# Two of each four gate rows on ScalarE, as gate * relu(1 - |column - slot|)

## The chip, the cores and the metric

The kernel runs on one core of one Trainium2 chip. The metric is device microseconds of one execution; lower is better. TensorE (PE) multiplies, VectorE (DVE) and ScalarE (ACT) work element by element, GpSimd (POOL) and SyncE (SP) here mostly start DMAs.

## The reference, cut to what matters

Two transformer blocks over 256 tokens of width 2048 are computed in float32. The second ends in a PEER layer: 8 heads choose 16 of 16,384 experts for each token (an expert number is a pair of key numbers from 0 to 127), and the chosen experts' outputs are summed with a softmax gate.

```python
def peer_ffn(h, w_pq, sub_keys, u_tab, v_tab):
    ...
    best, ci = lax.top_k(cand, PEER_TOPK)
    e1 = jnp.take_along_axis(i1, ci // PEER_TOPK, axis=-1)
    e2 = jnp.take_along_axis(i2, ci % PEER_TOPK, axis=-1)
    expert = (e1 * N_KEYS + e2).reshape(T, PEER_HEADS * PEER_TOPK)
    gate = jax.nn.softmax(best, axis=-1).reshape(T, PEER_HEADS * PEER_TOPK)
    ...
        act = jax.nn.gelu(jnp.einsum('cd,ckd->ck', hc, u), approximate=False) * gc
        vv = jnp.take(v_tab, ec, axis=0)
        return jnp.einsum('ck,ckd->cd', act, vv)
```

## The kernel before

The kernel gathers no experts. It computes all 16,384 of them in 8 groups of 16 tiles and multiplies each by a dense gate, which is zero for the experts that a token did not choose. The dense gates are built before that, in the gate loop, which is the subject here.

**What one group of the gate loop does.** For each token there are 128 chosen slots, one on each partition. `slot_T` holds them with the token along the free axis: part 0 is the first key number, part 1 the second, part 2 the gate. For a token, `hot_col` (128 slots x 128 columns) is 1 where the column equals key part 1, and `hot_row` is the gate where the column equals key part 0. Their product, a 128x128 matmul over the slots, is the token's 128x128 matrix of gates. The loop takes four tokens at a time, so it has 64 groups (n = 0 to 63), and everything in it is written out, not looped at run time:

- VectorE makes `hot_col[n % 2]` for four tokens in one instruction (L2214) and then the four `hot_row` rows in four instructions (L2219), each a comparison with one column of `slot_T` as a scalar and a multiplication by another. The last raises `hot_ready`. From n = 2 on it first waits for `hot_used`, that is until the matmuls of group n - 2 have read the same buffer.
- TensorE waits for `hot_ready` and for ScalarE's copy of group n - 2, runs four float32 matmuls (L1032; the trace counts eight, two passes each) into bank 3 or 4, and raises `hot_used`. While n is under 48 it then does one k-tile of an early expert tile (`whole_tiles`, L995, two passes) before the next group.
- ScalarE waits for `hot_used` and copies the bank to `g_stage` (L1408). After n = 15, 31 and 47 it also does the Gelu of an early expert tile (L1390). After n = 40 and n = 56 it splits two halves of a weight chunk into its high part (`split`, L1066, two instructions of 128x1024), and VectorE takes the low part of these after its groups n = 44 and 60 (`lower`, L1490, two instructions of 128x1024).
- GpSimd stores `g_stage` to DRAM every eight groups (L1473). When the last store has landed it loads the gates of the first expert group to `g_now` (L1477). VectorE's first product in the expert loop, `p_raw` (L2227), waits for that.

Ahead of the loop TensorE transposes the slots (L1021) and ScalarE copies them from the banks to `slot_T` in two instructions (L1399 and L1402). After the loop TensorE goes on with two chunks of the expert loop for which the weights are ready, and then waits for the chain that begins with `g_now`.

Each engine carries out its own instructions in the order written. The order across engines is set by semaphores only.

Of the kernel before, what the change touches and what calls it, by code (L numbers as in the profile page):

```python
# [9 lines left out]
ACT = mybir.ActivationFunctionType  # L10
# [3 lines left out]
P = 128  # L14
T = 256
# [170 lines left out]
def build(nc, a, out):  # L186
    with ExitStack() as ctx:
        def sb(name, shape, dt=F32, at=ctx):
            return at.enter_context(nc.sbuf_tensor(name, shape, dt))

        def sem(name):
            return ctx.enter_context(nc.semaphore(name))
# [15 lines left out]
        part = ExitStack()  # L208
        proj = sb("proj", [P, 44, T], at=part)
        bias = sb("bias", [P, HEADS1, T], at=part)  # L210
# [57 lines left out]


        sb("acc_again", [P, DT, T], at=part)  # L270
        slot_T = sb("slot_T", [P, 3, T], at=part)
        count = sb("count", [P, P + K_TOP], at=part)
        hot_row = [sb(f"hot_row{j}", [P, 4, P], at=part) for j in range(2)]
        hot_col = [sb(f"hot_col{j}", [P, 4, P], at=part) for j in range(2)]
# [27 lines left out]
        bank = [ctx.enter_context(nc.psum_tensor(f"bank{j}", [P, 512], F32)) for j in range(8)]  # L302
# [32 lines left out]
        sub_loaded, count_loaded, s3_done, acc_zero = (  # L335
            sem("sub_keys_loaded"), sem("count_loaded"), sem("scores3"), sem("acc_zero"))
        bank_read, best_ready, gate_exp, slots_done, slots_turned, turned_copied = (
            sem("scores3_read"), sem("best_less_max"), sem("gate_exp"), sem("slots_done"),
            sem("slots_transposed"), sem("slots_copied"))
        hot_ready, hot_used, gates_copied = sem("hot_ready"), sem("hot_used"), sem("gates_copied")  # L340
        gates_stored, g_loaded = [sem(f"gates_stored{j}") for j in range(2)], sem("gates_loaded")
        p_hi_done, p_lo_done = sem("p_hi_done"), sem("p_lo_done")
        cst2_loaded, dve_step, shift_step = sem("cst2_loaded"), sem("dve_step"), sem("shift_step")
# [29 lines left out]
        def pc(name, i=0, n=1):  # L373
            return par[:, PCOL[name] + i:PCOL[name] + i + n]
# [112 lines left out]
        def _(pe):  # L487
# [499 lines left out]
            def whole_tiles(x, k0, k1):  # L987

                c = N_PEER + x
                for k in range(k0, k1):  # L990
                    if k == 0 and x >= 2:
                        pe.wait_ge(gelu_done, FFN_Q * FQT + x - 1)
                    if k % 8 == 0:
                        pe.wait_ge(raw_loaded[c % 2][k // 8], 16 * (c // 2 + 1))
                    last = nc.tensor.matmul(bank[c % 2][:, 0:T], raw[c % 2][:, k * P:(k + 1) * P], h_f32[:, k, :],  # L995
                                            start=(k == 0), stop=(k == DT - 1))
                    if k % 8 == 7:
                        last.then_inc(half_done, 1)
# [27 lines left out]
            pe.wait_ge(turned_copied, 2)  # L1026
            for n in range(T // 4):
                pe.wait_ge(hot_ready, n + 1)
                if n >= 2:
                    pe.wait_ge(gates_copied, n - 1)  # L1030
                for x in range(4):
                    last = nc.tensor.matmul(bank[3 + n % 2][:, x * P:(x + 1) * P], hot_col[n % 2][:, x, :],  # L1032
                                            hot_row[n % 2][:, x, :], start=True, stop=True)
                last.then_inc(hot_used, 1)
                if n < (DT - EARLY) * DT:
                    whole_tiles(EARLY + n // DT, n % DT, n % DT + 1)
# [23 lines left out]
        def _(act):  # L1060
            def split(c, it, nk=DT):
                for part, (at, end) in enumerate(((0, HALF), (HALF, nk * P))):
                    act.wait_ge(raw_loaded[c % 2][part], it * 16 + (c // 2 + 1) * 16)
                    if c >= 2 or not isinstance(it, int):
                        act.wait_ge(half_done, it * 4 + (2 * c - 3 + part))
                    nc.scalar.activation(w_hi[c % 2][:, at:end], raw[c % 2][:, at:end], ACT.Copy  # L1066
                                         ).then_inc(hi_done, 1)
# [177 lines left out]
            for qh in range(16):  # L1245
# [4 lines left out]
                for tt in range(TT):  # L1250
                    x = 2 * qh + tt
                    nc.scalar.activation(prob2[qh % 2][:, tt, :], bank[3 + qh % 2][:, tt * T:(tt + 1) * T], ACT.Exp,
                                         bias=soft2[:, 0, x:x + 1], scale=0.125,
# [134 lines left out]
            def whole_gelu(x):  # L1388
                act.wait_ge(half_done, 2 * (N_PEER + x) + 2)
                nc.scalar.activation(u_act[:, x, :], bank[(N_PEER + x) % 2][:, 0:T], ACT.Gelu).then_inc(gelu_done, 1)  # L1390
# [9 lines left out]
                                 ).then_inc(turned_copied, 1)  # L1400
            act.wait_ge(slots_turned, 2)
            nc.scalar.activation(slot_T[:, 2, :], bank[6][:, 0:T], ACT.Copy).then_inc(turned_copied, 1)  # L1402
            for n in range(T // 4):
                b, at = n // 8, 4 * (n % 8)
                if b >= 2 and at == 0:
                    act.wait_ge(gates_stored[b % 2], 16 * (b // 2))
                act.wait_ge(hot_used, n + 1)
                nc.scalar.activation(g_stage[b % 2][:].rearrange("p g t e -> p t g e")[:, at:at + 4],  # L1408
                                     bank[3 + n % 2][:].rearrange("p (t g e) -> p t g e", t=4, e=K_TOP), ACT.Copy
                                     ).then_inc(gates_copied, 1)  # L1410
                if n % DT == DT - 1 and n < (DT - EARLY) * DT:
                    whole_gelu(EARLY + n // DT)
                if n in (FIRST_SPLIT, FIRST_SPLIT + 16):
                    split(N_PEER + DT + (n - FIRST_SPLIT) // 16, 0)
# [70 lines left out]
        def _(dve):  # L1485
# [7 lines left out]
            def lower(c, it, nk=DT, whole=0):  # L1493
                for part in range(2):
                    lower_part(c, it, part, nk, whole)
# [304 lines left out]
            n = prep.step(nc.vector.tensor_tensor(shift_c, pc("mu_prev", 0, 30), pc("mu_next", 0, 30), ALU.add))  # L1800
# [5 lines left out]
            n = prep.step(nc.vector.tensor_scalar(half_rk, pc("r_k", 0, 8), 0.5, None, ALU.mult))  # L1806
# [37 lines left out]
            for p in range(5):  # L1844
                if p + 1 < 5:
                    qk_mean(p + 1)
                x = proj2[:, 30 + 2 * p:32 + 2 * p, :]
# [23 lines left out]
            for qh in range(16):  # L1871
                m, x = qh // 2, 2 * qh
# [18 lines left out]
            for p in range(4):  # L1891
                x, ms = proj2[:, 30 + 2 * p:32 + 2 * p, :], q_ms[p % 2]
# [8 lines left out]
            def running_sum(m, d):  # L1901
                dve.wait_ge(affine_done, 2 * m + 1)
                return rw.step(nc.vector.tensor_tensor_scan(quad[1][:, d, :], reset, sig_w[:, d, :], 0.0,
                                                            ALU.mult, ALU.add))
# [22 lines left out]
            def kd_rows(m):  # L1927
                kd = bk[m % 3][:, 1, :, :]
                return rw.step(nc.vector.tensor_tensor(kd, kd, twice_of(8 + m), ALU.mult))
# [100 lines left out]
            for t in range(10):  # L2030
# [5 lines left out]
                for k in range(1, 6):  # L2036
# [3 lines left out]
                    if prepare and k == 1:  # L2040
                        n = running_sum(t, 1)
# [16 lines left out]
                    if prepare and k == 2:  # L2058
                        n = kd_rows(t)
# [30 lines left out]
            for p in range(4):  # L2090
# [3 lines left out]
                x, ms = proj2[:, 2 * p:2 * p + 2, :], q_ms[p % 2]  # L2094
# [3 lines left out]
                for t in (2 * p, 2 * p + 1):  # L2098
                    n = gn.step(nc.vector.tensor_scalar(proj2[:, t, :], proj2[:, t, :], pc("lnx_w", t), pc("lnx_b", t),
                                                        ALU.mult, ALU.add))  # L2100
# [110 lines left out]
            for n in range(T // 4):  # L2211
                if n >= 2:
                    dve.wait_ge(hot_used, n - 1)
                nc.vector.tensor_tensor(  # L2214
                    hot_col[n % 2][:], count[:, 0:P].unsqueeze(1).to_broadcast([P, 4, P]),
                    slot_T[:, 1, 4 * n:4 * n + 4].unsqueeze(2).to_broadcast([P, 4, P]), ALU.is_equal)
                for x in range(4):
                    t = 4 * n + x
                    last = nc.vector.tensor_scalar(hot_row[n % 2][:, x, :], count[:, 0:P], slot_T[:, 0, t:t + 1],  # L2219
                                                   slot_T[:, 2, t:t + 1], ALU.is_equal, ALU.mult)  # L2220
                last.then_inc(hot_ready, 1)
                if n in (FIRST_SPLIT + 4, FIRST_SPLIT + 20):
                    lower(N_PEER + DT + (n - FIRST_SPLIT) // 16, 0, whole=WHOLE)
# [150 lines left out]
```

## Time and profile before

| | |
|---|---|
| median of 3 runs | 4003.99 us (3989.61 to 4004.86) |
| the profiled execution's own time | 3994.76 us |
| its span in the profile | 3993.1 us |
| PE busy, share of the span | 3600.8 us, 90% |
| DVE busy | 2446.0 us, 61% |
| ACT busy | 1565.3 us, 39% |
| mean granted clock of TensorE | 0.939 of full speed |

Times are microseconds from the start of the span unless marked ns. PE is TensorE's matmuls and PEld its weight loads. Busy shares are means over stages with different limits. The gate loop lies between about 2498 and 2611.5 us, about 2.8% of the span, so what it costs is read from the rows of that stretch. The clock is given as a share of full speed: 1.0 is 2.4 GHz and 0.5 is 1.2 GHz.

### The profile page before, as it was taken

How to read it: one execution, taken by the hardware profiler on the slowest of the kernel's cores; microseconds unless marked ns; L12 is line 12 of the kernel's file. 1: busy time of each engine (PE TensorE's matmuls, PEld its weight loads, DVE VectorE, ACT ScalarE, POOL GpSimd, SP SyncE). 2: the span in 40 equal slices, each digit the busy share in tenths (PEclk: the TensorE clock that was granted, in tenths of full speed). 3: DMA queues.
4: the chain of work that ended last, by engine and by line, in shares of the span. 5: the costliest groups of instructions: out<-in, count | busy, mean ns of one | idle time of the engine just before them, and what ended most of it. 6: DMA issues, size and time to landing. Idle time of an engine off the chain costs nothing.

```text
span 3993.1 us, 71400 instructions
## 1 busy us (share of the span) xinstructions
PE 3600.8 (90%) x24910; PEld 3065.3 (77%) x24910; DVE 2446.0 (61%) x4140; ACT 1565.3 (39%) x2369; POOL 25.3 (1%) x40
## 2 busy tenths in 40 slices
PE   7996979999999799557786899889999999999998
PEld 5884768888888688236774787678888888888887
DVE  3464567676766675446554549955656565655665
ACT  3443344444444344232222330344535444444543
POOL 0000000000000000000000000000000000000000
PEclk8996989999999899559998999999999999999999
DMA  4551335556555355000000354456566565656564
GB/s 171 185 183 38 111 107 176 192 171 198 171 200 169 125 188 182 3 8 11 8 35 21 127 184 133 169 189 212 189 203 214 181 215 184 210 186 212 191 200 136
DMA packets 166200, 597.54 MB, mean 150 GB/s; under 512 B 18320, under 2 KB 26640, under 8 KB 164688
## 3 DMA queue, kind: packets, MB, share of 16 engines
q1 hardware_dynamic: 159600, 559.10, 43.0%
q0 software_dynamic: 6496, 36.96, 2.5%
q8 instruction: 76, 1.25, 0.1%
q14 instruction: 28, 0.23, 0.0%
HBM read 574.76 MB, written 20.97 MB: 149 GB/s over the span
## 4 chain that ended last, share of the span: by engine, by line
PE 81%; DVE 12%; ACT 3%; issue 2%; DMA 2%; DVEq 0%; SPq 0%; ACTq 0%; POOL 0%; POOLq 0%
PE bank L500 46%; PE bank L502 23%; PE bank L752 6%; DVE hot_row L2219 2%; PE bank L523 2%; DVE hot_col L2214 1%; PE bank L740 1%; PE bank L714 1%; PE bank L763 1%; DVE quad L1540 0%; ACT w_hi L1066 0%; PE bank L730 0%; DMA g_now<-gates 0%; DVE q_ms L1850 0%; DVE h_two L1530 0%
## 5 line engine op out<-in xcount | busy, mean ns | idle before, releaser
L500 PE MATMUL bank<-h_two,w_hi 128*128 128x512 f32 x5616 | 1973.2, 396 | 54.3 <-DVE h_two L1530 29.8
L502 PE MATMUL bank<-h_two,w_lo 128*128 128x256 f32 x5616 | 1576.7, 281 | 0.0
L1490 DVE TENSOR_TENSOR w_lo<-raw,w_hi 128x1024 fp32r<-128x1024 f32 (+1 forms) x1054 | 1224.8, 1185 | 224.0 <-ACT w_hi L1066 218.3
L500 PEld LDWEIGHTS bank<-h_two,w_hi 128*128 128x128 f32 x5616 | 1059.3, 189 | 304.6 <-issue 37.4
L1066 ACT ACTIVATE w_hi<-raw 128x1024 fp32r<-128x1024 f32 (+1 forms) x1054 | 1045.3, 1025 | 563.8 <-PE bank L502 524.5
L502 PEld LDWEIGHTS bank<-h_two,w_lo 128*128 128x128 f32 x5616 | 1067.6, 190 | 0.0
L500 PE MATMUL bank<-p_two,w_hi 128*128 128x512 f32 x1792 | 629.5, 394 | 2.5 <-DVE acc L1508 1.3
L502 PE MATMUL bank<-p_two,w_lo 128*128 128x256 f32 x1792 | 500.0, 279 | 0.0
L500 PEld LDWEIGHTS bank<-p_two,w_hi 128*128 128x128 f32 x1792 | 335.8, 187 | 86.8 <-DVE p_two L2233 5.6
L502 PEld LDWEIGHTS bank<-p_two,w_lo 128*128 128x128 f32 x1792 | 335.9, 187 | 0.0
L1504 DVE TENSOR_TENSOR acc<-acc,bank 128x256 f32 x192 | 81.0, 422 | 393.9 <-PE bank L502 393.9
L1071 ACT ACTIVATE stage<-bank 128x256 f32<-128x256 f32 x242 | 93.1, 385 | 479.7 <-PE bank L502 479.3
L500 PE MATMUL bank<-f_two,w_hi 128*128 128x512 f32 x704 | 252.0, 399 | 12.0 <-DVE f_two L1756 12.0
L1500 DVE TENSOR_TENSOR stage<-stage,bank 128x256 f32<-128x256 f32 x242 | 101.9, 421 | 218.7 <-ACT stage L1071 199.6
L502 PE MATMUL bank<-f_two,w_lo 128*128 128x256 f32 x704 | 201.8, 287 | 0.0
L500 PEld LDWEIGHTS bank<-f_two,w_hi 128*128 128x128 f32 x704 | 135.8, 193 | 42.3 <-DVE f_two L1756 13.2
L502 PEld LDWEIGHTS bank<-f_two,w_lo 128*128 128x128 f32 x704 | 136.6, 194 | 0.0
L995 PE MATMUL bank<-h_f,raw 128*128 128x256 f32 x512 | 120.1, 380 | 0.0
L523 PE MATMUL bank<-quad,cst 128*128 128x256 f32 x224 | 65.3, 462 | 51.0 <-ACT quad L1094 51.0
L995 PEld LDWEIGHTS bank<-h_f,raw 128*128 128x128 f32 x512 | 93.4, 191 | 10.4
L523 PEld LDWEIGHTS bank<-quad,cst 128*128 128x128 f32 x224 | 52.5, 238 | 63.1 <-ACT quad L1094 41.6
L1427 ACT ACTIVATE u_act<-stage 128x256 f32 x112 | 46.9, 419 | 136.2 <-DVE p_raw L2227 136.2
(328 smaller groups left out, 2865.5 us busy)
## 6 DMA issues: line engine op xcount, KB each, us to landing
raw<-in_u_tab SPq DMA_DIRECT2D x256, 512.0 KB, 3.9
raw<-in_v_tab SPq DMA_DIRECT2D x256, 512.0 KB, 4.4
raw<-in_w_up SPq DMA_DIRECT2D x176, 512.0 KB, 4.9
raw<-in_w_in SPq DMA_DIRECT2D x174, 512.0 KB, 4.3
raw<-in_w_out SPq DMA_DIRECT2D x64, 512.0 KB, 4.4
raw<-in_w_down SPq DMA_DIRECT2D x64, 512.0 KB, 3.5
raw<-in_w_pq SPq DMA_DIRECT2D x32, 512.0 KB, 4.4
gates<-g_stage POOLq DMA_DIRECT2D x8, 2048.0 KB, 8.5
```

Source lines behind the costliest of these rows:

```text
L500: nc.tensor.matmul(o[:], wh, two[:, k, :, :].rearrange("p a t -> p (a t)"), start=(k == 0), stop=False)
L502: last = nc.tensor.matmul(o[:, T:2 * T], wl, two[:, k, 0, :], start=False, stop=(k == nk - 1))
L523: last = nc.tensor.matmul(bank[2][:, 0:T], ones, quad[g % 2][:, k, :], start=(g == 0 and k == 0), stop=(g == groups - 1 and k == 3))
L752: return nc.tensor.matmul(o, lhs, rhs, start=start, stop=stop)
L995: last = nc.tensor.matmul(bank[c % 2][:, 0:T], raw[c % 2][:, k * P:(k + 1) * P], h_f32[:, k, :], start=(k == 0), stop=(k == DT - 1))
L1066: nc.scalar.activation(w_hi[c % 2][:, at:end], raw[c % 2][:, at:end], ACT.Copy).then_inc(hi_done, 1)
L1071: nc.scalar.activation(dst, bank[c % 2][:, 0:T], ACT.Copy).then_inc(copied, 1)
L1427: nc.scalar.activation(tile_of(u_act, i * 2 + j), stage[j][:], ACT.Gelu).then_inc(gelu_done, 1)
L1490: nc.vector.tensor_tensor(w_lo[c % 2][:, at:end], raw[c % 2][:, at:end], w_hi[c % 2][:, at:end].bitcast(F32), ALU.subtract).then_inc(lo_do ...
L1500: nc.vector.tensor_tensor(dst, dst, bank[c % 2][:, T:2 * T], ALU.add).then_inc(drained, 1)
L1504: nc.vector.tensor_tensor(dst, dst, bank[c % 2][:, 0:T], ALU.add).then_inc(acc_upper, 1)
L2219: last = nc.vector.tensor_scalar(hot_row[n % 2][:, x, :], count[:, 0:P], slot_T[:, 0, t:t + 1], slot_T[:, 2, t:t + 1], ALU.is_equal, ALU.mult)
```

## The change

Of each four rows of `hot_row`, VectorE keeps tokens x = 0 and 1. ScalarE builds x = 2 and 3, each in two instructions: `off = |column - slot|` (Abs, with the slot number as a bias read from `slot_T`, and scale -1) and then `relu(gate - gate * off)` (Relu, with a scale and a bias that are both read from `slot_T`). Since column and slot are whole numbers this is the gate where they are equal and zero elsewhere. A fourth part of `slot_T` holds the negated gate, from one more copy of the bank. The new semaphore `off_done` is raised by each of these instructions: ScalarE waits on it between its own steps, and TensorE waits for it before each group. ScalarE makes the rows of groups 0 and 1 ahead of its loop, and those of group n + 2 after its copy of group n.

```diff
-        slot_T = sb("slot_T", [P, 3, T], at=part)
+        slot_T = sb("slot_T", [P, 4, T], at=part)
+        off = sb("off", [P, 2, P], at=part)
...
+        off_done = sem("off_done")
...
             for n in range(T // 4):
                 pe.wait_ge(hot_ready, n + 1)
+                pe.wait_ge(off_done, 4 * n + 4)
...
             nc.scalar.activation(slot_T[:, 2, :], bank[6][:, 0:T], ACT.Copy).then_inc(turned_copied, 1)
+            nc.scalar.activation(slot_T[:, 3, :], bank[6][:, 0:T], ACT.Copy, scale=-1.0).then_inc(turned_copied, 1)
+            act.wait_ge(count_loaded, 16)
+            act.wait_ge(turned_copied, 3)
+
+            def gate_rows(n):
+
+                if n:
+                    act.wait_ge(off_done, 4 * n)
+                for x in (2, 3):
+                    t = 4 * n + x
+                    nc.scalar.activation(off[:, x - 2, :], count[:, 0:P], ACT.Abs, scale=-1.0, bias=slot_T[:, 0, t:t + 1]
+                                         ).then_inc(off_done, 1)
+                for x in (2, 3):
+                    t = 4 * n + x
+                    act.wait_ge(off_done, 4 * n + x - 1)
+                    nc.scalar.activation(hot_row[n % 2][:, x, :], off[:, x - 2, :], ACT.Relu,
+                                         scale=slot_T[:, 3, t:t + 1], bias=slot_T[:, 2, t:t + 1]).then_inc(off_done, 1)
+
+            gate_rows(0)
+            gate_rows(1)
             for n in range(T // 4):
...
                                      ).then_inc(gates_copied, 1)
+                if n + 2 < T // 4:
+                    gate_rows(n + 2)
...
-                for x in range(4):
+                for x in range(2):
                     t = 4 * n + x
                     last = nc.vector.tensor_scalar(hot_row[n % 2][:, x, :], count[:, 0:P], slot_T[:, 0, t:t + 1],
                                                    slot_T[:, 2, t:t + 1], ALU.is_equal, ALU.mult)
```

## Rows read from the trace of the kernel before

**Rows 1.** The page's chain that ended last, by engine

```profile
PE 81%; DVE 12%; ACT 3%; issue 2%; DMA 2%; DVEq 0%; SPq 0%; ACTq 0%; POOL 0%; POOLq 0%
```

**Rows 2.** The chain in order of time, 2494 to 2635: start, us, what

```profile
2512.70 0.60 DVE hot_col L2214
2513.30 1.03 DVE hot_row L2219 x4
...
2573.57 2.27 DVE w_lo L1490 x2
...
2611.91 7.50 DMA gates<-g_stage
...
2620.01 8.02 DMA g_now<-gates
```

**Rows 3.** Groups of instructions in 2497.5 to 2611: busy us, mean ns, idle before

```profile
L2219 DVE TENSOR_SCALAR hot_row<-count,slot_T 128x128 f32<-128x128 f32 x256 | 72.0, 356 | 0.0
...
L2214 DVE TENSOR_TENSOR hot_col<-count,slot_T 128x512 f32<-128x512 f32 x64 | 43.9, 686 | 3.5 <-ACT slot_T L1402 2.1 <-PE bank L1032 1.4
L1408 ACT ACTIVATE g_stage<-bank 128x512 f32<-128x512 f32 x64 | 38.2, 597 | 70.9 <-PE bank L1032 70.9
...
L1390 ACT ACTIVATE u_act<-bank 128x256 f32<-128x256 f32 x3 | 1.1, 378 | 0.0
```

**Rows 4.** Timeline of the gate loop: start us, us, engine, line, work

```profile
2497.61 0.38 ACT L1402 ACTIVATE slot_T<-bank 128x256 f32<-128x256 f32 x1
...
2501.97 0.60 ACT L1408 ACTIVATE g_stage<-bank 128x512 f32<-128x512 f32 x1 [3.98 <-PE bank L1032]
...
2504.47 0.60 ACT L1408 ACTIVATE g_stage<-bank 128x512 f32<-128x512 f32 x1 [1.90 <-PE bank L1032]
...
2509.50 1.16 PE L1032 MATMUL bank<-hot_row,hot_col 128*128 128x128 f32 x8
...
2511.13 0.97 PEld L1032 LDWEIGHTS bank<-hot_row,hot_col 128*128 128x128 f32 x8 [0.44 <-DVE hot_row L2219]
...
2568.74 1.99 ACT L1066 ACTIVATE w_hi<-raw 128x1024 fp32r<-128x1024 f32 x2
...
2610.87 0.60 ACT L1408 ACTIVATE g_stage<-bank 128x512 f32<-128x512 f32 x1 [0.51 <-PE bank L1032]
```

**Rows 5.** ScalarE's groups over the whole span, forms apart

```profile
L1313 ACT ACTIVATE rb<-bank 128x128 f32<-128x128 f32 x32 | 8.9, 278 | 70.0 <-PE bank L752 70.0
...
L1287 ACT ACTIVATE sig_w<-bank,small 128x256 f32<-128x256 f32 x16 | 6.7, 471 | 22.3 <-PE bank L763 22.3
...
L1297 ACT ACTIVATE bk<-sig_a,small 128x512 f32<-128x512 f32 x8 | 6.5, 813 | 0.3
...
L1304 ACT ACTIVATE decay<-quad 128x512 f32<-128x512 f32 x8 | 5.0, 619 | 0.0
...
L1141 ACT ACTIVATE prob<-logit,soft 128x128 f32<-128x128 f32 x8 | 3.1, 393 | 0.2 <-DVE soft L1602 0.2
...
L1390 ACT ACT_TABLE_LOAD x2 | 2.6, 1283 | 0.0
```

**Rows 6.** ScalarE's timeline where instructions follow each other

```profile
1781.31 0.84 ACT L1287 ACTIVATE sig_w<-bank,small 128x256 f32<-128x256 f32 x2 [9.24 <-PE bank L763]
...
1785.19 0.81 ACT L1297 ACTIVATE bk<-sig_a,small 128x512 f32<-128x512 f32 x1
1785.90 0.61 ACT L1304 ACTIVATE quad<-quad 128x512 f32<-128x512 f32 x1
...
1844.93 0.56 ACT L1320 ACTIVATE uv<-bank 64x128 f32<-64x128 f32 x2 [1.16 <-PE bank L752]
```

**Rows 7.** Engines' busy time by stretch; TensorE's granted clock is third from last

```profile
2500.00:2504.00 4.00, 4.00 (x17) 3.82 (x18) 3.09 (x10) 0.60 (x1) 0.00 (x0) 0.50 0.01 4
...
2584.00:2598.00 14.00, 10.03 (x70) 8.51 (x71) 14.00 (x44) 5.71 (x10) 0.89 (x1) 1.00 0.76 272
```

## The prediction

> **What bounds the kernel now.** I read the chain that ended last first. By engine it is mostly TensorE, with 12% of VectorE [rows 1]. The chain in order of time shows where the edited lines stand in it: from about 2504 to 2607 us it is VectorE alone, `hot_col` and four `hot_row` instructions in turn [rows 2]. So in the gate loop VectorE sets the pace and the other engines follow. One group takes 0.60 + 1.03 = 1.63 us there, which is 0.257 us for each `hot_row` instruction. VectorE's low parts, 2.27 us for a pair, are in the chain too, twice. Behind the loop stand the store of the gates (7.50 us) and the load of `g_now` (8.02 us) [rows 2]. Whatever moves the last copy to `g_stage` moves these, and with them the end.
>
> The groups of instructions in the stretch show how much room the others have. VectorE has 3.5 us of idle time before `hot_col`. ScalarE is idle for 70.9 us, always until TensorE's matmuls are done, and its 64 copies take 597 ns each [rows 3]. TensorE is not far from its own limit: the gap in its weight loads is 0.44 us in a group of 1.63 [rows 4], so a group with its expert tile needs about 1.19 us at full clock.
>
> **The change on VectorE.** Two of four rows go: 2 x 0.257 = 0.51 us for a group, which leaves 1.11 us. TensorE's work does not change. If nothing else bound the loop, it would now run at some 1.2 us a group.
>
> **The change on ScalarE.** It adds four instructions of 128x128 to a group. The trace has no Abs and no Relu, so I price them by form.
> - Abs reads SBUF, with a bias that is read from a tile. The nearest form is L1141, an Exp of 128x128 from SBUF with such a bias: 393 ns [rows 5].
> - Relu has a scale and a bias that are both read from a tile. L1297 is such an instruction at 128x512: 813 ns. L1304, the same shape without either, takes 619 ns [rows 5]. Each operand of this kind therefore costs 97 ns, and Relu takes 393 + 97 = 490 ns.
> - Instructions that follow each other overlap. Two of L1287 at 471 ns each [rows 5] span 0.84 us, and L1304 begins 0.71 us after the start of an L1297 that lasts 0.81 [rows 6]. The overlap is 0.10 us in both, with operands from tiles. So the spacing is 0.29 us for Abs, 0.39 for Relu and 0.50 for the copy of 0.597.
> - The waits on `off_done` cost nothing in a steady group: the first Relu starts 0.58 us after the first Abs, which was done at 0.39; the second Relu needs the second Abs (done at 0.68) and starts at 0.97.
>
> A group on ScalarE: 0.50 + 2 x 0.29 + 2 x 0.39 = 1.86 us. That is more than VectorE's 1.63 was. **ScalarE becomes the bound of the loop**, and each group is 0.23 us longer than before. TensorE's 1.19 us and VectorE's 1.11 us lie below it. Nor does the ring of waits bind: the rows of group n + 2 are ready 1.96 us after the copy of group n began, the matmuls take 1.16 [rows 4], and 3.2 us for two groups is under 2 x 1.86.
>
> The Trainium skill has a price and a rule here ("ScalarE: Activation LUTs", sections "What ACT_TABLE_LOAD costs" and "Rules for kernel authors"). The price is 186 ns + 0.833 ns per column, 93 ns more for each operand from a tile, and 93 ns of overlap; an estimate by it is 1.88 us for the group, which would put 1 us on the sum. The rule sends relu, max, add and mul to VectorE; its ratio is stated for bf16, which no row here shows, but in float32 a row costs VectorE 0.257 us and would cost ScalarE 0.68.
>
> **Edits that cost nothing, and what hides them.** The extra copy to `slot_T` and the rows of groups 0 and 1 lie ahead of ScalarE's loop. The copies of groups 0 and 1 begin 2.50 us apart in before, at half clock [rows 4, 7], and the first begins 4.4 us after L1402. On ScalarE, the copy (0.38), two sets of rows at 1.46 us each and the waits between end at 2501.3, before the first group's matmuls do at about 2501.9. Group 0's rows are ready at 2497.61 + 0.28 + 0.38 + 0.03 + 1.46 = 2499.8, and its matmuls, which take some 2 us at half clock and end at 2501.9, need them about then. If this cover were gone it would cost about a microsecond, once. TensorE's extra wait costs nothing while its group is shorter than ScalarE's.
>
> VectorE's two low parts (4.5 us in before) go off the path: VectorE now idles 0.75 us a group, its rows are 1.2 us early, and the copy behind the matmuls has 0.5 us of slack, together more than 2.27. In their place ScalarE's own work is no longer hidden: two splits at 1.99 - 0.10 = 1.89 us [rows 4] and three Gelus at 0.378 - 0.10 = 0.28 us [rows 3], in all 3.8 + 0.8 = 4.6 us.
>
> **The sum**, from the start of L1402 to the end of the last copy. Before: 2610.87 + 0.60 - 2497.61 = 113.9 us [rows 4].
> - to the copy of group 1, set by TensorE at half clock: 2504.47 - 2497.61 = 6.9 us, unchanged
> - 60 groups to the copy of group 61: 60 x 1.86 = 111.6
> - splits and Gelus: 4.6
> - from there the rows of group 63 (1.96), its matmuls (1.16), its copy (0.60) and handovers: 3.8
>
> After: 126.9 us. The difference is +13.0 us, or 0.33%. Store and load follow unchanged, and TensorE's idle time ahead of `g_now` moves with them. Against the profiled execution's 3994.76 us this gives 4007.8. That execution lies 9.2 us under the median of the runs, so against the median I forecast **4017 us**.
>
> **The bounds.** Everything hangs on the spacing of ScalarE's small instructions, which counts 60 times. Low: if operands from tiles added nothing once pipelined, each would be spaced like the plain 128x128 of L1313, 0.278 - 0.10 = 0.18 us [rows 5]; ScalarE's group would be 1.22 us. High: no overlap at all, as in the two of L1320 that span 0.56 us [rows 6], with full durations 0.60 + 2 x 0.39 + 2 x 0.49 and small gaps: 2.45 us. I take 1.86, since the rows with such operands show the overlap, and L1320 writes other partitions in each of its two.
>
> **The rivals.**
> - *Faster (0.07).* Spacing at the low bound. Then TensorE and the handovers set about 1.22 us: 6.9 + 73.2 + 4.6 + 3.1 = 87.8, which is 26 us less, 3978 us. For it: VectorE is the bound, and half its row work goes. Against it: L1297 and L1287 keep their longer spacing. It decides below a spacing sum of 1.63 us for ScalarE's group; to be faster by over 0.5% it needs 1.32.
> - *The overlap is lost at the waits (0.14).* Three of ScalarE's four new instructions stand behind a wait on ScalarE's own semaphore, which no row shows with the wait already met. At 2.45 us a group: 60 x 0.59 = 35 us on top, 4052 us. From 1.98 us a group it is slower by over 0.5%.
> - *The clock falls (0.08).* TensorE works 1.16 us in a group of 1.86 from n = 48 on, 62%, where it was busy for 72% at full clock before [rows 7]. At half clock a group with its expert tile takes 2.50 us [rows 4]. Half the time at that clock until n = 47 adds 24 x 0.64 = 15 us: 4032. Against it: at 2.50 us TensorE is busy throughout, and the clock returns.
> - *Table loads (0.03).* A load is 1283 ns [rows 5]. If Abs and Relu needed another table than Gelu, the three Gelus would cost six loads, 8 us more (4025); if they needed one each, 128 loads, 164 us (4181). The skill's page (same title, section "Table sets: the hidden batching unit") states that relu and abs are in every set. No run here shows it yet.
> - *My forecast* has the remaining 0.68.
>
> **How the numbers follow.** About 0.5% (20 us) is what a measurement of this kernel can tell from no change. The forecast is +13 us with some 7 us either way from the spread of the runs, and leaves about 0.10 of its 0.68 beyond +20 us. Slower: 0.10, 0.13 of the lost overlap, 0.05 of the clock, 0.02 of the tables: 0.30. Faster 0.06. Within 0.5%: 0.64. The range of 8 in 10 runs from 4000, the forecast less the spread and a group of 1.75 us (-7 us), to 4040, which takes in the clock and two thirds of the lost overlap. The forecast alone spans 4006 to 4028.
>
> **What would show it.** In the profile of the changed kernel: ScalarE busy nearly throughout 2504 to 2624, copies to `g_stage` 1.86 us apart, Abs near 390 and Relu near 490 ns; the chain through ScalarE's rows in place of VectorE's; VectorE idle before `hot_col` for over 40 us; the low parts out of the chain and the splits in it; the last store of the gates 13 us later; no table load in the loop. Copies 1.2 us apart, or 2.4, or a clock of 0.5 in the loop would prove me wrong.

## The result

| | median | runs |
|---|---|---|
| before | 3999.48 us (3989.61 to 4007.9) | 12 |
| after | 4013.51 us (3999.14 to 4020.0) | 12 |

The ratio is 1.0032, with a 95% interval of 1.0018 to 1.0045. At 4000 us that is 13 us slower (7 to 18). The forecast was +13.0 us.

**The profile after.** The page's busy line and its chain by engine and line, to be read beside [rows 1]:

```profile
PE 3607.2 (90%) x24910; PEld 3071.3 (77%) x24910; DVE 2417.4 (60%) x4012; ACT 1645.8 (41%) x2626; POOL 25.0 (1%) x40
...
PE 81%; DVE 10%; ACT 6%; issue 2%; DMA 2%; DVEq 0%; SPq 0%; ACTq 0%; POOL 0%; POOLq 0%
PE bank L502 45%; PE bank L504 23%; PE bank L754 5%; PE bank L525 2%; ACT hot_row L1421 1%; ACT off L1416 1%; PE bank L742 1%; PE bank L716 1%; ACT g_stage L1431 1%; ACT w_hi L1069 1%; PE bank L765 1%; DVE quad L1565 0%; DMA g_now<-gates 0%; PE bank L732 0%; DVE q_ms L1875 0%
```

VectorE lost 2 points of the chain and ScalarE won 3. VectorE's busy time fell by 28.6 us and ScalarE's rose by 80.5 us: work left the engine that set the pace of the gate loop, and more than that arrived on another. The chain in order of time, in the steady part of the loop (start, us, what), answers to [rows 2]:

```profile
2512.65 0.48 ACT g_stage L1431
2513.13 0.58 ACT off L1416 x2
2513.71 0.77 ACT hot_row L1421 x2
2514.48 0.48 ACT g_stage L1431
...
2582.89 1.89 ACT w_hi L1069 x2
...
2629.11 7.49 DMA gates<-g_stage
...
2637.19 8.73 DMA g_now<-gates
```

Where `hot_col` and `hot_row` of VectorE stood, every piece is now ScalarE's: copy 0.48, two Abs 0.58, two Relu 0.77, together 1.83 us a group. The split of a weight chunk stands in the chain, VectorE's low parts do not. The waits in the stretch of the loop (who waited for whom: us in total, times, longest) show the slack of the others:

```profile
DVE hot_col L2239 <- PE bank L1035: 41.5, 60, 1.7
...
ACT g_stage L1431 <- PE bank L1035: 2.6, 6, 0.8
```

ScalarE's wait ahead of its copies fell from 70.9 us [rows 3] to 2.6. VectorE waits 41.5 us for TensorE, where it had waited 1.4 of its 3.5 us [rows 3].

**How the runs are compared.** The two profiled executions differ by 21.1 us, but the code ahead of the loop is the same in both and already differs by 4.6 us: L1402 of before, L1405 of after, starts at 2497.61 and at 2502.19. In the experiments below it starts anywhere from 2487.8 to 2507.4. From the end of the last copy to the end of the span it is 1381.6 us before and 1385.5 after, and between 1381.7 and 1384.4 in the experiments, without relation to how long their loops are. So from a profile I use only the length of the loop, from that start to the end of the last copy, and for the whole kernel the ratio of many runs. The loop took 113.9 us before and 2628.66 - 2502.19 = 126.5 us after, 12.6 us more.

### The profile page after: what moved, and what is told of

It reads as the page before. It is cut to its first block, busy times and chain, and to the rows that moved or that the text cites. A ratio compares the mean times of both kernels' runs of the same rounds, so it can differ in the third digit from the quotient of the medians.

```text
span 4014.2 us, 71531 instructions
## 1 busy us (share of the span) xinstructions
PE 3607.2 (90%) x24910; PEld 3071.3 (77%) x24910; DVE 2417.4 (60%) x4012; ACT 1645.8 (41%) x2626; POOL 25.0 (1%) x40
## 4 chain that ended last, share of the span: by engine, by line
PE 81%; DVE 10%; ACT 6%; issue 2%; DMA 2%; DVEq 0%; SPq 0%; ACTq 0%; POOL 0%; POOLq 0%
PE bank L502 45%; PE bank L504 23%; PE bank L754 5%; PE bank L525 2%; ACT hot_row L1421 1%; ACT off L1416 1%; PE bank L742 1%; PE bank L716 1%; ACT g_stage L1431 1%; ACT w_hi L1069 1%; PE bank L765 1%; DVE quad L1565 0%; DMA g_now<-gates 0%; PE bank L732 0%; DVE q_ms L1875 0%
## 5 line engine op out<-in xcount | busy, mean ns | idle before, releaser
L1069 ACT ACTIVATE w_hi<-raw 128x1024 fp32r<-128x1024 f32 (+1 forms) x1054 | 1045.3, 1025 | 564.1 <-PE bank L504 522.4
L1035 PEld LDWEIGHTS bank<-hot_row,hot_col 128*128 128x128 f32 x512 | 67.4, 204 | 47.6 <-issue 46.1
L1035 PE MATMUL bank<-hot_row,hot_col 128*128 128x128 f32 x512 | 77.0, 297 | 28.0 <-issue 19.8
```

## The experiments

The spacing is that of the copies to `g_stage` in the steady part. It and the loop length are from each kernel's one profiled execution; the ratios are of 4 to 12 runs of each kernel against 12 to 24 of before.

| kernel | us a group | loop, us | against before's loop | timed ratio (95% interval) |
|---|---|---|---|---|
| before | 1.63 | 113.9 | | |
| after | 1.83 | 126.5 | +12.6 | 1.0032 (1.0018 to 1.0045) |
| one row on ScalarE | 1.37 | 101.8 | -12.1 | 0.9965 (0.9955 to 0.9976) |
| three rows | 2.51 | 167.4 | +53.5 | 1.0118 (1.0104 to 1.0133) |
| Relu with immediates | 1.46 | 105.4 | -8.5 | 0.9972 (0.9960 to 0.9983) |
| third row on VectorE, unused | 1.83 | 126.3 | +12.4 | 1.0028 (1.0018 to 1.0039) |
| four more met waits | 1.83 | 126.7 | +12.8 | 1.0029 (1.0018 to 1.0040) |
| one row, Abs ahead | 1.37 | 100.9 | -13.0 | 0.9959 (0.9945 to 0.9972) |
| rows on both, ScalarE's unused | 1.83 | 124.3 | +10.4 | 1.0021 (1.0012 to 1.0031) |

In every row but one the loop's difference lies inside the interval of the timed ratio. With three rows it is 53.5 us, and the interval ends at 53.2. So the gate loop accounts for the differences as far as these runs can tell.

**One row on ScalarE.**

```diff
-                for x in (2, 3):
+                for x in (3,):
...
-                for x in range(2):
+                for x in range(3):
```

(twice in ScalarE's part, once in VectorE's; `off` and the counts of `off_done` follow)

> ScalarE makes one row of each four (x = 3), VectorE three. If ScalarE's spacing sets the loop of the changed kernel: ScalarE needs about 0.48 + 0.37 + 0.39 = 1.24 us a group (Relu must now wait for the only Abs ahead of it), VectorE 0.60 + 3 x 0.257 = 1.37 us, TensorE 1.19, so VectorE sets the pace again. The loop from the second copy to slot_T to the last copy takes 6.7 + 60 x 1.37 + 4.5 (low parts) + 3.3 = about 97 us, against 113.9 before and 126.5 with two rows: about 17 us or 0.4% faster than before. Rival, the handovers to ScalarE and the extra wait on TensorE cost the time, however many rows: still 1.8 us a group, slower than before. Rival, VectorE's rows do not matter at all: 1.63 us and no change.

The pace is VectorE's again, at 1.37 us, and the kernel is 0.35% faster than before. The loop is 5 us longer than I worked out. Three lines of its chain tell where half of that went:

```profile
2581.04 0.56 ACT g_stage L1431
...
2582.04 13.87 DMA gates<-g_stage
...
2595.93 0.60 ACT g_stage L1431
```

The store of eight groups took 13.87 us, and eight groups now take only 8 x 1.37 = 11. ScalarE had to wait 2.5 us for the buffer. In before the same store took 12.9 us, ScalarE came back to its buffer 13.7 us after the store began, and nobody waited. Of the rest, part is TensorE's clock, which is granted at 0.62 from 2596 to 2602, right after that wait; I did not take the remainder apart.

**Three rows on ScalarE.** The same edit with `(1, 2, 3)` and `range(1)`.

> ScalarE makes three rows of each four (x = 1 to 3), VectorE one. If each row costs ScalarE the spacing of an Abs and a Relu (0.29 + 0.385): 0.48 + 3 x 0.675 = 2.51 us a group, the loop about 167 us, 41 us more than with two rows and 54 us (1.3%) more than before. Rival, a fixed cost of the handover: 1.84 us stays, 0.3% slower than before.

2.51 us a group and a loop of 167.4 us, both as worked out. From two rows to three a group is 0.68 us longer, which is the price of a row: 0.29 for the Abs and 0.385 for the Relu. A fixed cost of the handover as the cause of the loss is ruled out.

**Relu with immediates.**

```diff
-                                         scale=slot_T[:, 3, t:t + 1], bias=slot_T[:, 2, t:t + 1]).then_inc(off_done, 1)
+                                         scale=-1.0).then_inc(off_done, 1)
```

> All instructions and waits of the changed kernel stay, but the Relu takes scale -1 and no bias instead of two operands read from slot_T, so the rows x = 2 and 3 hold no gates. If operands from tiles cost 97 ns each in the spacing: Relu is spaced 0.19 us instead of 0.385, a group takes 0.48 + 0.58 + 0.38 = 1.45 us, and the loop is 25 us shorter than with two rows, 12 us (0.3%) faster than before. Rival, the count of instructions and waits sets the spacing: 1.84 us a group stays, and 0.3% slower than before.

The timeline of ScalarE, first in the kernel after, then here:

```profile
2592.70 0.58 ACT L1431 ACTIVATE g_stage<-bank 128x512 f32<-128x512 f32 x1
2593.17 0.69 ACT L1416 ACTIVATE off<-count,slot_T 128x128 f32<-128x128 f32 x2
2593.76 0.87 ACT L1421 ACTIVATE hot_row<-off,slot_T 128x128 f32<-128x128 f32 x2
2594.53 0.58 ACT L1431 ACTIVATE g_stage<-bank 128x512 f32<-128x512 f32 x1
```

```profile
2531.24 0.63 ACT L1431 ACTIVATE g_stage<-bank 128x512 f32<-128x512 f32 x1
2531.72 0.74 ACT L1416 ACTIVATE off<-count,slot_T 128x128 f32<-128x128 f32 x2
2532.30 0.55 ACT L1421 ACTIVATE hot_row<-off 128x128 f32<-128x128 f32 x2
2532.70 0.63 ACT L1431 ACTIVATE g_stage<-bank 128x512 f32<-128x512 f32 x1
```

The starts are what to read. From the first Relu to the next copy, which is two Relus, it is 0.77 us with two operands from `slot_T` each and 0.40 us with none. So each operand costs (0.77 - 0.40) / 4 = 0.09 us of spacing. The number of instructions and waits is the same. With these operands the change is slower than before; without them, which leaves wrong gates in two of four rows, it is faster (0.9972). The loop came out 4 us longer than expected: a group took 1.46 us, a store was waited for (1.4 us), and groups 1 to 2 and 58 to 59 were 2.1 and 2.3 us apart.

**A third row on VectorE, unused.**

```diff
+                nc.vector.tensor_scalar(spare[:, n % 2, :], count[:, 0:P], slot_T[:, 0, 4 * n:4 * n + 1],
+                                        slot_T[:, 2, 4 * n:4 * n + 1], ALU.is_equal, ALU.mult)
```

> The changed kernel, and VectorE makes a third row of 128x128 again, into a tile that nobody reads. VectorE then has 1.37 us a group. If ScalarE sets the pace with 1.84 us, nothing changes: 1.84 us a group, 0.3% slower than before, VectorE idle 0.26 us less in each group. If VectorE or the ring through it still sets the pace, 0.257 us more in each of 64 groups, 16 us, 0.7% slower than before.

Nothing changes. VectorE's own timeline shows the row going into its idle time, which falls from 0.63 us a group in the kernel after to 0.37:

```profile
2530.42 0.69 DVE L2239 TENSOR_TENSOR hot_col<-count,slot_T 128x512 f32<-128x512 f32 x1 [0.63 <-PE bank L1035]
```

```profile
2531.48 0.69 DVE L2240 TENSOR_TENSOR hot_col<-count,slot_T 128x512 f32<-128x512 f32 x1 [0.37 <-PE bank L1036]
2532.09 0.34 DVE L2243 TENSOR_SCALAR spare<-count,slot_T 128x128 f32<-128x128 f32 x1
2532.35 0.60 DVE L2247 TENSOR_SCALAR hot_row<-count,slot_T 128x128 f32<-128x128 f32 x2
```

**More waits.** Ahead of each Abs and each Relu:

```diff
+                    act.wait_ge(count_loaded, 16)
```

> The changed kernel, and ahead of each Abs and each Relu of ScalarE one more wait, on a semaphore that has long been raised: four more waits a group. If waits that are met cost ScalarE nothing behind running instructions: 1.84 us a group as in the changed kernel, 0.3% slower than before. If they break the overlap of its instructions (0.1 us each) or take a turn of their own: 0.1 to 0.4 us more a group, 6 to 25 us, 0.5 to 0.9% slower than before.

1.83 us a group and the same loop. Four waits that are already met add nothing to the spacing here. That waits break the overlap was the largest of my rivals.

**ScalarE's rows made but not used.** VectorE makes all four rows (`range(4)`), TensorE's new wait on `off_done` is left out, and the Relu writes elsewhere:

```diff
-                    nc.scalar.activation(hot_row[n % 2][:, x, :], off[:, x - 2, :], ACT.Relu,
+                    nc.scalar.activation(spare[:, n % 2, x - 2, :], off[:, x - 2, :], ACT.Relu,
```

> VectorE makes all four rows as in the kernel before. ScalarE does the Abs and the Relu of two rows as well, but into a tile that nobody reads, and TensorE does not wait for it. If what counts is that ScalarE's instructions stand in one stream with its copies to g_stage: ScalarE's 1.84 us a group sets the pace all the same, the loop takes 126 us, 0.3% slower than before, as in the changed kernel. If the loss comes from the handover of the rows to TensorE or from its added wait: 1.63 us a group and the time of the kernel before. If taking rows off VectorE had still bought something: slower than the changed kernel.

Again 1.83 us a group, though no engine waits for the rows and VectorE has its old load. The waits in the loop now name the copy as what TensorE lacks:

```profile
PE bank L1035 <- ACT g_stage L1431: 21.1, 49, 2.6
```

So the loss comes through ScalarE's stream: its 1.35 us of rows stand between one copy and the next, and TensorE needs the copy to reuse its bank. This kernel has twice the rows of the kernel after on VectorE and one wait less on TensorE, and its groups take the same time: what was taken off VectorE bought nothing. The loop is 2.2 us shorter than after's. Its start is not (6.8 us to the copy of group 1, against 6.7), but its copies stay 1.83 us apart behind the splits, where those of after are up to 2.3 apart, which makes 1.5 us, and from the copy of group 61 to the end it takes 3.0 us against 3.8, as its last two copies follow each other with no matmul to wait for.

**One row, with the Abs a group ahead.** ScalarE's order after the copy of group n becomes the Relu of group n + 2 and then the Abs of group n + 3.

```diff
+                if n + 2 < T // 4:
+                    gate_row(n + 2)
+                if n + 3 < T // 4:
+                    distance(n + 3)
```

> One row on ScalarE as before, but its Abs is issued a group ahead, so that Relu never waits for the Abs directly in front of it. ScalarE then needs 0.48 + 0.29 + 0.39 = 1.16 us a group, VectorE still 1.37. If VectorE sets the pace with one row, nothing is won beyond 1 or 2 us where ScalarE catches up after its splits: ratio 0.996 to 0.997, as with one row. If ScalarE's wait for its own Abs sets the pace with one row: 0.08 us less a group, 5 us more gained.

The group stays at 1.37 us, so ScalarE's wait for its own Abs did not set the pace. The loop is 0.9 us shorter, and the ratio of 0.9959 cannot be told from that of one row. Its median is the lowest measured here, and it is faster than both given kernels. It waits 3.0 us for the store of the gates:

```profile
ACT g_stage L1433 <- DMA gates<-g_stage: 3.0, 1, 3.0
```

## Why the prediction was right

**The bound.** VectorE set the loop's pace before, and ScalarE does after, by its number of instructions and their spacing. One, two and three rows gave 1.37, 1.83 and 2.51 us a group; worked out were 1.37, 1.86 and 2.51. Only the 1.86 was worked out before any result; the other two used spacings measured in the kernel after. A third row on VectorE that nobody uses, and all four rows on VectorE beside ScalarE's load, show that VectorE's share has no effect once ScalarE sets the pace.

**The price of the operations the trace lacked.** Abs was priced by an Exp of the same shape with the same kind of bias, Relu by the step from an instruction with immediates to one with two operands from a tile at another width. Forecast spacings were 0.29 and 0.39 us; measured are 0.58 / 2 = 0.29 and 0.77 / 2 = 0.385. The copy was 0.48, not 0.50, which makes 1.83 of 1.86. The overlap held, as the rows of pairs with such operands said [rows 6]. The pair of L1320 that showed none was rightly set aside, though no run shows why it has none. The estimate by the Trainium skill ("ScalarE: Activation LUTs", section "What ACT_TABLE_LOAD costs"), 1.88 us, was 0.05 above.

**The hidden and the exposed work.** The chain has the splits on the path and no low part. The low parts were free, as forecast, but the splits cost more than their own 1.89 us: while ScalarE splits, TensorE runs out of rows, and its clock falls just after. At the second split TensorE waits 2.60 us for ScalarE's row. VectorE ends its low part at 2619.81, and even then it waits 1.17 us for TensorE before it can go on:

```profile
2618.90 3.88 PE L1035 MATMUL bank<-hot_row,hot_col 128*128 128x128 f32 x16 [2.60 <-ACT hot_row L1421]
...
2620.98 0.69 DVE L2239 TENSOR_TENSOR hot_col<-count,slot_T 128x512 f32<-128x512 f32 x1 [1.17 <-PE bank L1035]
```

At the first split TensorE waits 2.16 us in the same way. The windows of the kernel after (third from last is the granted clock) show what follows:

```profile
2512.00:2582.00 70.00, 59.17 (x380) 45.03 (x379) 45.85 (x114) 70.00 (x193) 4.51 (x5) 1.00 0.44 159
...
2588.00:2592.00 4.00, 4.00 (x24) 3.77 (x24) 2.36 (x6) 3.55 (x11) 0.00 (x0) 0.71 0.00 0
2592.00:2606.00 14.00, 9.34 (x64) 7.42 (x63) 9.17 (x24) 14.00 (x40) 0.89 (x1) 1.00 0.56 185
2606.00:2615.00 9.00, 5.65 (x40) 4.81 (x40) 5.87 (x16) 9.00 (x26) 0.89 (x1) 1.00 0.45 180
2615.00:2622.00 7.00, 4.23 (x22) 4.05 (x23) 5.20 (x11) 6.65 (x16) 0.00 (x0) 0.68 0.89 311
```

and the copies are further apart there:

```profile
2586.39 0.70 ACT L1431 ACTIVATE g_stage<-bank 128x512 f32<-128x512 f32 x1
...
2588.66 0.60 ACT L1431 ACTIVATE g_stage<-bank 128x512 f32<-128x512 f32 x1 [0.21 <-PE bank L1035]
...
2590.85 0.60 ACT L1431 ACTIVATE g_stage<-bank 128x512 f32<-128x512 f32 x1 [0.24 <-PE bank L1035]
```

2.27 and 2.19 us instead of 1.83, and 2.31 and 2.02 after the second split, together 1.5 us. This is the rival of the clock in small. In the steady part it did not come: the clock stayed at 1.0 from 2512 to 2582 and from 2592 to 2615, and in the last of these windows TensorE's matmuls are on for 5.65 of 9 us, 63%, where the prediction had 62%.

**The sum**, term by term: to the copy of group 1 it took 6.7 us (forecast 6.9); from there to the copy of group 61 it took 2624.85 - 2508.87 = 116.0 us (111.6 + 4.6 = 116.2), in which the shorter copy (60 x 0.03 = 1.8 us less) and the half clock behind the splits (1.5 us more) cancel; from there to the end 3.8 (3.8). In all 126.5 of 126.9.

**The rivals.** Faster: the spacing never fell to the plain instruction's. Waits that break the overlap: the two Relus, each behind its wait on `off_done`, are spaced 0.385 us, as without any loss, and four more waits changed nothing. Table loads: ScalarE's groups in the loop, L1416, L1421, L1431, L1393 and L1069, have no table load beside them. The Trainium skill's rule that relu, max, add and mul belong on VectorE (same title, section "Rules for kernel authors") agrees with the price of a row here, 0.257 us on VectorE against 0.68 on ScalarE, though in float32. It does not settle where a row should go: one row of four on ScalarE gains, two lose.

**What was luck.** The median of after, 4013.5, is 3.5 us below the 4017 forecast, since before's median over more runs is 4.5 us lower than the one shown. The ratio is what the forecast should be held to, and its interval of 7 to 18 us is too wide to tell 13.0 from a few us more or less. That 126.9 us came so near to 126.5 is luck too, in so far as the two errors above cancel; the half clock behind the splits was in no term of the sum.

## What to carry to other kernels

When work moves from one engine to another, add up both engines' spacing per round of the loop, with all that already stands in the receiver's stream, and move only as much as makes the two sums meet: here 1.63 against 0.48 us, with a row worth 0.257 us on the one and 0.68 on the other. One row in four gains 0.35% and two lose 0.32%. Price an instruction that the trace lacks by the rows of the same shape and the same kind of operands, not by its name. A loop that gets faster shortens the cover of what runs beside it: a store of 12.9 us with 13.7 us of cover was free, and one of 13.87 us with 11.4 us of cover was waited for.

## What the runs showed of the hardware

**Durations grew while the spacing stood still.** In the kernel after, the same pair of Abs is recorded with 0.68 us just after ScalarE has waited and with 0.80 us some 35 groups later, and the copy goes from 0.58 to 0.70. After the next wait both are short again:

```profile
2579.00 0.69 ACT L1431 ACTIVATE g_stage<-bank 128x512 f32<-128x512 f32 x1
2579.48 0.80 ACT L1416 ACTIVATE off<-count,slot_T 128x128 f32<-128x128 f32 x2
...
2580.84 0.69 ACT L1431 ACTIVATE g_stage<-bank 128x512 f32<-128x512 f32 x1
...
2591.34 0.68 ACT L1416 ACTIVATE off<-count,slot_T 128x128 f32<-128x128 f32 x2
```

The starts stay 1.83 or 1.84 us apart in the steady part. The means over the loop, 435 ns for Abs and 527 for Relu, are therefore above the 393 and 490 I had worked out, though the spacing is not. So in this loop, where ScalarE is never idle, the distance of the starts is the price, and the mean duration is not. Why the records stretch I did not find out; with three rows the copy reached 0.799 us.
